# The second layer's modulation, taken off TensorE's products: GpSimd and VectorE weigh the weight blocks, TensorE adds up partitions

## The reference, cut to what matters

```python
sc, scc = jax.nn.silu(c), jax.nn.silu(c_ctx)
for l in range(DEPTH):                      # DEPTH = 2
    mx = (sc @ w_mod[l] + b_mod[l]).reshape(b, 1, N_MOD, d)      # N_MOD = 6, d = 1024
    mz = (scc @ w_mod[l] + b_mod[l]).reshape(1, 1, N_MOD, d)
    hx = modulate(rmsnorm(x, norm_g[l, 0]), mx[:, :, 0], mx[:, :, 1])
    hz = modulate(rmsnorm(z, norm_g[l, 0]), mz[:, :, 0], mz[:, :, 1])
    ...                                     # mixer, feed-forward; parts 2 to 5 used likewise
    if not last: z = ...                    # in the last layer z takes parts 0 and 1 alone
```

## Time and profile before

| what | us |
|---|---|
| median of 3 runs | 2366.3 (2364.92 to 2380.07) |
| the profiled execution, whole | 2377.46 |
| its span (first to last instruction) | 2375.7 |
| steps of this stage, in the span | 1238 to 1406 |
| units of this stage | 1410 to 1506 |
| granted TensorE clock, mean share of full speed | 0.964 |

### The profile page before, as it was taken

The page is one execution under the profiler, slowest core; times in us unless marked ns, Lnnn a source line. Parts: engine busy times, 40 slices in busy tenths (PEclk is TensorE's granted clock), DMA queues, the critical chain, the costliest instruction groups (busy, mean ns, idle before and its releaser), DMA issues. The chain is left out here.

```text
span 2375.7 us, 39337 instructions
## 1 busy us (share of the span) xinstructions
PE 2195.6 (92%) x16530; PEld 1659.9 (70%) x16530; DVE 1406.9 (59%) x2680; ACT 542.7 (23%) x1209; POOL 242.7 (10%) x335
## 2 busy tenths in 40 slices
PE   4999989979998999999989999997898899999998
PEld 2556655558886855555558889785554588888998
DVE  3535856576672466665664533574676636778754
ACT  3103632422113321111110012111452032111111
POOL 2000100047750000000001100000110000000000
PEclk8999989989999999999999999998798899999999
DMA  8450011100004112112127777332000212333454
GB/s 307 142 195 19 1 32 47 29 2 4 4 4 142 37 48 59 53 54 71 54 73 250 230 220 209 106 86 67 1 1 18 71 36 73 87 89 89 134 171 140
DMA packets 235633, 205.10 MB, mean 86 GB/s; under 512 B 6771, under 2 KB 219458, under 8 KB 235266
## 3 DMA queue, kind: packets, MB, share of 16 engines
q1 hardware_dynamic: 222050, 157.07, 22.2%
q0 software_dynamic: 12416, 42.32, 5.1%
q10 hardware_dynamic: 992, 3.21, 0.4%
HBM read 200.48 MB, written 2.10 MB: 85 GB/s over the span
## 5 line engine op out<-in xcount | busy, mean ns | idle before, releaser
L1546 PE MATMUL banks<-mem 128*128 128x384 f32 (+1 forms) x2296 | 622.1, 433 | 0.0
L1546 PEld LDWEIGHTS banks<-mem 128*128 128x128 f32 x2296 | 435.3, 190 | 186.3
L2333 PEld LDWEIGHTS banks<-mem 128*128 128x128 f32 x2464 | 279.9, 193 | 31.2 <-issue 24.5
L2333 PE MATMUL banks<-mem 128*128 128x128 f32 x2464 | 287.5, 278 | 15.0 <-PEq L1818 7.7
L1893 PE MATMUL banks<-mem 128*128 128x256 f32 (+1 forms) x672 | 181.1, 426 | 8.7 <-issue 4.0
L1893 PEld LDWEIGHTS banks<-mem 128*128 128x128 f32 x672 | 128.9, 194 | 60.3 <-issue 21.3
L1740 DVE TENSOR_TENSOR mem<-mem,banks 128x384 f32<-128x384 f32 (+1 forms) x287 | 131.2, 487 | 43.2 <-PE banks L1546 40.5
L1486 PE MATMUL banks<-mem 128*128 128x256 f32 x640 | 144.7, 388 | 10.7 <-PEq L1377 8.6
L683 PE MATMUL banks<-mem 128*128 128x384 f32 x448 | 146.4, 486 | 2.1 <-PEq L429 1.4
L985 PE MATMUL banks<-mem 64*64 64x64 f32 x3840 | 127.7, 221 | 18.5 <-DVE mem L1261 11.4
L1486 PEld LDWEIGHTS banks<-mem 128*128 128x128 f32 x640 | 123.9, 195 | 29.8 <-issue 11.5
(11 more groups left out here) (384 smaller groups left out, 2901.2 us busy)
## 6 DMA issues: line engine op xcount, KB each, us to landing
mem<-in_ffn_w_up SPq DMA_DIRECT2D x88, 512.0 KB, 4.4
mem<-in_w_mod POOLq DMA_DIRECT2D x48, 512.0 KB, 5.0
mem<-in_w_mod POOLq DMA_DIRECT2D x16, 1024.0 KB, 7.1
mem<-in_ffn_w_down SPq DMA_DIRECT2D x32, 512.0 KB, 5.0
mem<-in_ab_w_in SPq DMA_DIRECT2D x24, 512.0 KB, 5.1
mem<-in_ffn_w_down SPq DMA_DIRECT2D x16, 768.0 KB, 6.1
mem<-in_ffn_w_down SPq DMA_DIRECT2D x16, 704.0 KB, 7.7
mem<-in_ffn_w_down SPq DMA_DIRECT2D x16, 640.0 KB, 5.4
```

The lines of the kernel that those rows point to most:

```text
L1546: last = nc.tensor.matmul(fast.out(i, name), weights[:, k, :], tokens[:, k, :], start=k == 0, stop=k == 3)
L2333: last = c.nc.tensor.matmul(self.out(name), rows(k), weights[:, k - lo, :], start=k == 0, stop=k == 10)
```

## The change

The 48 side products go. In their place the two operands are multiplied elementwise where they lie, one scalar of `sc` for each partition, and summed over the eight blocks k; what is left for TensorE is to add up the 128 partitions, with the stationary operand `unit` (columns [1,0] for the first stream's sum, [0,1] for the second's). The six parts become twelve halves m of 512 columns:

- **GpSimd, halves 0 to 3** (parts 0 and 1, both streams): for each block two `tensor_scalar` and, from the second block on, two `tensor_tensor` additions, all 128x512. In all 64 of the first and 56 of the second kind, 16 pairs of blocks, 16 further issues of loads between them. It waits on itself behind nearly every one.
- **VectorE, halves 4 to 11** (parts 2 to 5, image alone): eight operations of 128x512 a half (one `tensor_scalar`, seven `scalar_tensor_tensor`), 64 in all: four each in steps 6 and 7 and in units 0 to 13.
- **TensorE**: a reduction for each half, of four matmuls of 256 columns where there are two sums (m < 4), of two where there is one; at the places of `REDUCE_AT` (step or 8 for the units, product or unit number).
- **Loads**: again 48 of 512 KB from GpSimd's queue, now two blocks of 512 columns each. While VectorE weighs, load q waits for the blocks of load q-2.
- **Drains** follow the reductions; ScalarE waits for the first two at step 4, since the sums of halves 0 and 1 stand where step 4 writes.

```diff
     def behind_product(self, pe, s, n):
-        if n % 5 == 0 and n:
-            self.side_product(pe, 4 * s + n // 5 - 1)
+        self.side_reduction(pe, s, n)
...
+    TWO_ROWS, ONE_ROW = 4, 8
+    REDUCE_AT = ((2, 0), (3, 16), (5, 6), (7, 6), (8, 0), (8, 2), (8, 4), (8, 6), (8, 8), (8, 10), (8, 12), (8, 14))
...
+    def side_reduction(self, pe, s, n):
+        if (s, n) in self.REDUCE_AT:
+            m = self.REDUCE_AT.index((s, n))
+            if m % 2 == 0 and m:
+                pe.wait_ge(self.mod_drained, m // 2)
+            if m < self.TWO_ROWS:
+                pe.wait_ge(self.pool_summed, m + 1)
+            else:
+                pe.wait_ge(self.dve_weighed, KT * (m - self.TWO_ROWS + 1))
+            self.side.sum_partitions(m % 2, self.side_sums(m), self.side_bank(m // 2)).then_inc(self.mod_used, 1)
...
+    def weigh_on_pool(self, pool):
...
+        for q in range(4 * self.TWO_ROWS):
...
+            pool.wait_ge(self.mod_in[q % 2], 16 * (q // 2 + 1))
+            for k in (2 * (q % 4), 2 * (q % 4) + 1):
+                w = self.side_weights(m, k)
+                x_to, z_to = sums if k == 0 else (self.weighed, w)
+                g.tensor_scalar(x_to, w, c.sc[:, k, 0:1], None, ALU.mult).then_inc(self.pool_weighed, 1)
+                pool.wait_ge(self.pool_weighed, done + 1)
+                g.tensor_scalar(z_to, w, c.sc[:, k, 1:2], None, ALU.mult).then_inc(self.pool_weighed, 1)
+                done += 2
+                if k:
+                    g.tensor_tensor(sums[0], sums[0], self.weighed, ALU.add).then_inc(self.pool_weighed, 1)
+                    pool.wait_ge(self.pool_weighed, done)
+                    g.tensor_tensor(sums[1], sums[1], w, ALU.add).then_inc(self.pool_weighed, 1)
+                    done += 2
+                pool.wait_ge(self.pool_weighed, done)
...
+            self.load_side(pool, q + 2)
+        for q in range(4 * self.TWO_ROWS + 2, 4 * (self.TWO_ROWS + self.ONE_ROW)):
+            pool.wait_ge(self.dve_weighed, 2 * (q - 1 - 4 * self.TWO_ROWS))
+            self.load_side(pool, q)
+
+    def weigh_on_dve(self, dve, first, last):
...
+            dve.wait_ge(self.mod_in[q % 2], 16 * (q // 2 + 1))
+            if k == 0:
+                dve.wait_ge(self.pool_summed, self.TWO_ROWS)
+                dve.wait_ge(self.mod_used, m - 1 if m > self.TWO_ROWS + 1 else self.TWO_ROWS if m > self.TWO_ROWS else 1)
+                ins = v.tensor_scalar(to, w, c.sc[:, k, 0:1], None, ALU.mult)
+            else:
+                dve.wait_ge(self.dve_weighed, n)
+                ins = v.scalar_tensor_tensor(to, w, c.sc[:, k, 0:1], to, ALU.mult, ALU.add)
...
             for s in range(pairs.STEPS):
+                if s == pairs.PER_GROUP:
+                    act.wait_ge(pairs.mod_used, 2)
...
-                if s % 2:
-                    pairs.drain(dve, s // 2)
+                if s == 4:
+                    pairs.drain(dve, 0)
+                if s >= 6:
+                    pairs.weigh_on_dve(dve, 4 * (s - 6), 4 * (s - 5))
+                if s == 7:
+                    pairs.drain(dve, 1)
...
+                if q < 14:
+                    pairs.weigh_on_dve(dve, 8 + 4 * q, 12 + 4 * q)
```

68 lines of the change are left out of this document (46 added, 22 removed).

## The result

| | us, median of 4 | lowest to highest | ratio to before, 95% interval |
|---|---|---|---|
| before | 2368.6 | 2364.9 to 2380.1 | |
| after | 2462.3 | 2453.4 to 2468.7 | 1.0369 (1.0333 to 1.0405) |

The changed kernel is 94 us slower by the medians and 87 us by the ratio. The forecast was 34 us slower, 2400, in a range that ended at 2430. The direction was right and the size was not. The profiled execution of the changed kernel took 2455.9 us, its span is 2454.1.

A forecast was written before the change was run, and what follows sets the result against it. It took TensorE to pace the stage. Steps +14 us (with the -17.3 saving inside), second drain +2.8, units +12 and clock +6 made +35, said as +34: 2400 us against the 2366.3 median, range 2366 to 2430.

The forecast's parts named there:

- What bounds the kernel: Steps and units: TensorE sets the stage's pace, busy 164 of 168 us and 96 of 96.
- What the change takes off the path, -17.3 us: TensorE in steps and units: 48 side products save 25.9 us, twelve reductions cost 8.6, net -17.3.
- no contention in the steps: Rival: GpSimd and VectorE do not hold each other up in the steps; 2371 us, chance 0.12.
- The price of the scaling, 0.61 us: GpSimd's 128x512 tensor_scalar in the steps costs the same as its copy, 0.61 us, 64 times.
- the scaling costs like an addition: Rival: GpSimd's scaling costs 1.27 us, 42 us more in all, 2442 us; chance 0.15.
- Turn-taking: Steps: GpSimd's operations and VectorE's two-memory-operand ones alternate whole, half 3 ready at 1404 to 1407, steps +14 us.
- holds: Steps: time per operation that cannot overlap the other engine's; VectorE 62 us, GpSimd 95, together 157 before half 3.
- the scalings take no turn: Rival: in the steps only GpSimd's additions take turns with VectorE, holds fall by 31 us; 2390 us, chance 0.15.
- The second drain, +2.8 us: Entry to the units: VectorE weighs four blocks ahead of the drain TensorE waits on, 4 x 0.69 = +2.8 us.
- Units, +12 us: Units: loads through two buffers, 7.2 us a round against 5.11 a unit, make 108.6 us instead of 96.6.
- Clock, +6 us, bounds 0 to 12: Step 4 and late units: two further drops to half clock after TensorE's waits, +6 us, 0 to 12.
- The sum: Whole kernel: 14 + 2.8 + 12 + 6 = +35, said as +34; forecast 2400 us.

The follow-up runs named there:

- e12: Kernel before with 24 of the steps' 32 side products shrunk to one matmul of 8 columns, nothing added; 0.9995 of before.
- e4: Changed kernel with GpSimd's arithmetic cut to copying the first block into each of the two sums, loads kept; 1.0080 of before.
- e3: Changed kernel with halves 0 to 3 back on TensorE as 16 side products, GpSimd only issuing loads; 1.0083 of before.
- e5: e3 without 28 of GpSimd's loads and the waits for them, VectorE weighing the same two pairs of blocks repeatedly; 0.9981 of before.
- e2: Changed kernel with all 64 GpSimd scalings made plain copies; 2400.7 us, 1.0155 of before.
- e1: Changed kernel with GpSimd's scalings in another form per half: copy, tensor_scalar by constant, tensor_tensor with spread column, tensor_scalar by column; one run, 2447 us.
- e10: Changed kernel with GpSimd's 64 scalings written as tensor_tensor with the column spread over 512; 2448.9 us, 1.0311 of before.

## Why the prediction was wrong, step by step

**What bounds the kernel.** Wrong for the steps, right for the units. "Work taken off TensorE should count, if TensorE is what the stage waits for. The busy times by stretch say it is": e12 says it is not: 24 side products less, and the ratio is 0.9995. The busy share shows who works, and not who would work less long if the other hurried. There was a sign that I did not weigh: in the steps of the kernel before VectorE waits 53.5 us for w_down. Its sums come "just in time, with little slack", as the prediction has it, because the loads do.

**What the change takes off the path, -17.3 us.** About 13.0 of it lay in the steps (32 x 0.54 less four reductions of 1.08); measured there, 2.7 us (e4) and nothing (e12). Where 16 products went and nothing came in their place it was more, 5.4 us in e3 and 4.1 in e5, which have the same steps, for 8.6 worked out. These two, like e4, also move fewer bytes of `w_mod` in the steps (205 GB/s in all for e3, 200 for e4, 234 for before and e12), and no run parts the two. It did not spoil the forecast of the changed kernel, since there GpSimd sets the end of the steps. It would have spoiled that of the rival "no contention in the steps", 2371: e4_quiet_gpsimd, which is that rival made real, takes 1.008 of before, 19 us more where the rival had 5: its steps and the entry are together 1 us longer where the rival had 10 less; most of the rest is the units'.

**The price of the scaling, 0.61 us.** This is the step that failed. The miss is 62 us by the medians (2462 against 2400) and 53 by the ratio. 64 x 0.95 makes 61, but what the price was worth is measured by e2: 50 us, all in the steps. The other 10 are the units', below. The bounds that I gave, the copy's 0.61 and the addition's 1.27, did not hold it: 1.56. "One input and one output makes it like the copy" was a likeness in the number of operands, with the arithmetic left out. The rival "the scaling costs like an addition", which had 0.15, was the nearest in kind, and at 2442 too low.

Against that rival the prediction also named the Trainium skill, and there page and trace part: "GPSIMD Engine Reference", section "4.1 Engine selection", calls one-input operations on GpSimd roughly line-rate. For the copy the trace agrees (0.61 us), for tensor_scalar it does not (1.49 and 1.56 us, above the two-input addition's 1.26). The measurement decides.

**Turn-taking.** The mechanism is right. With the forecast's own price in the kernel (e2), half 3 is ready 165 us after the start of the steps (forecast 1404 to 1407, so 166 to 169), the halves are 37 to 42 us apart (39), the steps grow by 15.8 us (14). But the path is another: the sum lets half 3 set the end of the steps, and in e2 it lies ready 5 us early, while TensorE waits 18.2 us for subtractions. So that 14 came so near to 15.8 is partly luck. In the changed kernel half 3 does set the end. The count was a little off too: the sum puts all 96 subtractions ahead of half 3, but the last eight are queued behind it, 4 us of holds. With 1.56 in place of 0.61 the same sum of holds, 64 x 1.43 + 56 x 1.14 + 62 = 217 us, puts half 3 at 1464, or 1460 without those eight; it was ready at 1455.5. And one row did not fit the rule as I put it: VectorE's line 3716 has one operand in memory and was held all the same. That the one-input scalings take turns too, which no row of before showed, can be seen on GpSimd's first three in the changed kernel:

```profile
1247.25 1.67 POOL L2514 TENSOR_SCALAR mem<-mem 128x512 f32<-128x512 f32 x1 [2.94 <-DMA mem<-in_w_mod]
1249.02 2.11 POOL L2516 TENSOR_SCALAR mem<-mem 128x512 f32<-128x512 f32 x1
1251.22 2.32 POOL L2514 TENSOR_SCALAR mem<-mem 128x512 f32<-128x512 f32 x1
```

1.67, then 2.11 and 2.32 us where 1.56 is the undisturbed case. The rival "the scalings take no turn" is out.

**The second drain, +2.8 us.** Measured +3.7: TensorE waits 5.3 us for it, in the changed kernel and in every variant that keeps four weighings and their loads in front of it (e1, e2, e4, e10).

**Units, +12 us.** The mechanism, a chain of loads through two buffers, is right (e5), the size is not: +22. By the sum's own layout a round came to 8.0 us, (118.2 - 22.2) / 12, against 7.2. In the changed kernel's trace a buffer's round from 1514 on is 7.7 us on the mean: 5.4 from the start of its issue to its landing, 0.5 in which it lies there while VectorE is at other work, 1.5 of two weighings, and 0.3 until GpSimd issues again. The landing was a little shorter than the 5.7 that I took; what the sum lacks is VectorE's absence and most of GpSimd's wake-up, to which it gave 0.1. The eight loads before, issued from 1474.3 to 1505.3, take 9.9 us a round, 6.0, 2.1, 1.5 and 0.3: there VectorE's row norms (lines 2145 and 2148, 2.5 us each time) stand between the weighings, and VectorE waits only 1.3 us for loads before 1516 and 22.9 after. The sum named the row norms and gave them no time.

**Clock, +6 us, bounds 0 to 12.** 8.5 us in the steps (e4 against after, the same 1264 matmuls) and 6.6 in the units (98.0 against the 91.4 us of e5_no_unit_loads, 769 matmuls each), a part of it inside time that TensorE would have waited anyway. The low clock follows the waits: after each of the four waits of 11 to 17 us TensorE went on at half clock. Small beside the price of the scaling, and an effect of it.

**The sum.** In e2, the kernel that the prediction priced, the steps are 15.8 us longer for 14, the entry to the units 3.7 for 2.8, the units 20.8 for 12, and the 6 us of clock are inside these lengths: 40 for 35. By its ratio that kernel is 37 us slower than before, where 34 were forecast. So but for one price, and a chain of loads that was made too quick, the sum held in size, in the steps partly by luck.

## What to carry to other kernels

Before an operation that no row shows goes 64 times onto a path, its price is the first thing to measure, and a bound from "the nearest row" must come from the same kind of arithmetic, not from the same number of operands. Where two engines are both nearly always just in time, a busy share does not tell which of them paces the other: look at what the second one waits for, and take work away from the first alone to see what comes back. And work given to GpSimd beside a VectorE that works on two operands in memory is not parallel work: in this case the two engines' times added up. Look for such pairs before counting an engine as free.

## What the hardware showed that I had not expected

- On GpSimd, for 128x512 in float32: copy 0.61 us, tensor_tensor with one operand a spread column 1.04, of two full operands 1.26, tensor_scalar by a constant 1.49, by a column 1.56. tensor_scalar, with less to read than the addition, is the dearest. On ScalarE the same scaling is 0.72, on VectorE the multiply-and-add of the change 0.75 on the mean.
- A one-input operation of GpSimd and a two-operand one of VectorE hold each other up as two-input additions do (copy 0.61 up to 1.01 us, scaling 1.56 up to 2.50).
- The turns are not fair. With GpSimd's next operation ready each time, one subtraction of VectorE waited through four additions, 5.93 us for 0.69. It had started 0.45 us before the first of them, while GpSimd was issuing a load. The Trainium skill's page "SBUF — State Buffer", section "SBUF: two separate sides", gives the shared pair to whichever operation starts first; by the starts in this trace that was VectorE, and it waited. The measurement decides.
